# Hybrid attention and short-conv block on one core: keys held once, the normed input in a ring of slices, query tiles up and down in turn, merge from the last block

## The chip, the core and the metric

The kernel runs on one core of a Trainium2 chip. The metric is the device time of one execution in microseconds (us). Three timed runs of the kernel before gave 1969.12, 1975.21 and 1975.68 us, median 1975.21. TensorE (PE) does matrix products, VectorE (DVE) and ScalarE (ACT) work element by element, GpSimd (POOL) makes masks here, and SyncE (SP) issues every DMA, in order, from one program. Data lie in HBM, in on-chip SBUF (128 partitions) and in eight PSUM banks of 128 x 512 float32.

## The reference

```
h = RMSNorm(x)                                     # x: 2048 x 1024
q,k,v,z_att,b,c,u,z_conv,g_att,g_conv = split(h @ W_in)
A: 4 value heads; each has two query/key heads of width 64, partial rotary on q and k
   a = softmax(q1 k1^T / 8) - lam * softmax(q2 k2^T / 8), masked by position // 64
   att = RMSNorm(a @ v) * (1 - 0.2) * silu(z_att);      y_att = att @ W_att_out
B: y_conv = (b * conv3_causal(c * u) * silu(z_conv)) @ W_conv_out
m = sigmoid(g_att + bias0) * y_att + sigmoid(g_conv + bias1) * y_conv
out = x + RMSNorm(m @ W_out)
```

All is float32. Each operand of a large product is held as two reduced-precision parts, hi and lo (value minus hi), and a product is three matmuls: hi*hi, hi*lo, lo*hi. A score product packs the two parts into the 128 contracted rows (64 rows each), so two matmuls give all four part products.

## The kernel before, in words

The sequence has 4 blocks of 512 positions (NB) or 16 tiles of 128 (NT). There are four stages, and the order within each engine is fixed by the code.

1. **Norm and v.** x is loaded tile by tile (two buffers), normed, transposed by PE, split, and kept as `ht0` to `ht3`, one per block. w_v comes in four pieces through the two buffers `raw`. For each tile PE makes v (24 matmuls of 512 columns) and stores it to HBM.
2. **Projections.** 28 weight tiles `p` (z, conv, then q and k), each over the four blocks b = 0 to 3: 24 matmuls each (`split_product`), PSUM bank 4*(p%2)+b. ACT and DVE split the results, SP stores them (`qk_s`, `z_s`, `cv_s`). During the conv tiles, weights that are needed later are split into `split_s` in HBM: 16 gate tiles, 8 of the two output projections, 8 of W_out. `ht1` to `ht3` are stored to `ht_s`.
3. **Attention with gates between.** The work goes over TILES = 64 pairs (value head `pair`, query tile), G = 16*pair + tile, tiles upwards in every pair. Keys seen grow with the tile (`keys(G)`), in chunks of 512. In round R (-1 to 67) PE does the scores of G = R+1, the transposes of G = R-1, and in even rounds the product with v for two tiles. Between these steps stand *gate units* (`gates`, the fill): 64 units of 24 matmuls with h as the moving operand, whose results go to `gate_s`. `Plan` sets how many fill matmuls a round has, from column counts of PE (`tensor_columns`) and DVE (`vector_columns`). The first LEAD = 60 fill matmuls stand ahead of round -1. A unit needs its 1 MB weight (`w0`/`w1` in turn, loaded when the unit before the last is done) and h of its block, one buffer `ht0`: when block bb changes (units 16, 32, 48), `load_ht` reloads it in four pieces as the last unit frees them. `k_sl[c]` holds for each chunk the keys twice, in partitions 0-63 and again in 64-127, so one chunk takes 8 DMAs; `q_st` holds four tiles.
4. **Merge**, blocks b = 0 to 3. For m = 0 to 7 PE makes two half sums (`y_done`; 12 matmuls each, banks 0-3); gates come from HBM into `ring` (4 buffers), ACT takes the sigmoid, DVE multiplies, adds, ACT makes `m_hi` and DVE `m_lo`. Then 8 outputs of W_out (`f_done`; 24 matmuls each, banks 4-7), the norm, the residual and the store. `wa`, `br` (branch results) and `wo` are loaded after stage 3.

## Time and profile before

| | |
|---|---|
| median of three timed runs | 1975.21 us |
| profiled execution, and its span | 1981.93 us, 1980.1 us |
| PE busy | 1784.4 us (90%) in 8512 matmuls |
| DVE, ACT, POOL busy | 895.5, 583.5, 89.1 us |
| DMA | 345.66 MB, mean 175 GB/s |
| mean granted clock of PE | 0.953 of 2.4 GHz |

The span is first work to last work; 1.8 us of the profiled time lie around it. A busy share is an average: PE is the engine that is nearly always busy, so what counts is where it is idle and where its clock is at the lower level. "Idle before" or "waited for" names what ended an idle time.

### The profile page before, as it was taken

To read this page: it belongs to the slowest core of one execution; us is meant where nothing else is said; L and a number is where in the kernel's file an instruction comes from. 1 tells how busy PE (TensorE), PEld (TensorE's weight loads), DVE (VectorE), ACT (ScalarE), POOL (GpSimd) and SP (SyncE) were. 2 spreads that over 40 slices of the span, in tenths; PEclk is the share of its full clock that TensorE was granted. 3 is DMA by queue.
4 is the path that set the end of the run, shared out by engine and by line. 5 is a ranking of instruction groups with operands and counts; after the bars stand their busy time and mean duration, and the time that the engine had idled before them with its cause. 6 is when DMAs were issued, how large, how long until landed. Compare 5 with 4: busy or idle time off the path is not lost.

```text
span 1980.1 us, 22286 instructions
## 1 busy us (share of the span) xinstructions
PE 1784.4 (90%) x8512; PEld 1481.4 (75%) x8512; DVE 895.5 (45%) x1903; ACT 583.5 (29%) x1040; POOL 89.1 (5%) x74
## 2 busy tenths in 40 slices
PE   5999999999999992999899889978998279999998
PEld 4878888888888881788688778867887267777776
DVE  4546243535443310566466646744665032423232
ACT  5412112112112110344344434433444022323131
POOL 0000000000000000110111111101100000000000
PEclk8999999999999996999999989988999689999999
DMA  5557346566555349555864795497532944343432
GB/s 191 160 192 305 113 175 217 181 193 200 180 194 168 117 117 208 178 164 184 243 203 150 187 264 164 135 214 237 160 123 87 381 140 164 96 160 96 162 95 84
DMA packets 142853, 345.66 MB, mean 175 GB/s; under 512 B 14225, under 2 KB 51089, under 8 KB 127121
## 3 DMA queue, kind: packets, MB, share of 16 engines
q1 hardware_dynamic: 142738, 344.15, 55.6%
q8 instruction: 69, 1.13, 0.2%
q14 instruction: 46, 0.38, 0.1%
HBM read 224.55 MB, written 119.55 MB: 174 GB/s over the span
## 4 chain that ended last, share of the span: by engine, by line
PE 73%; DMA 12%; SPq 5%; ACT 4%; DVE 3%; issue 2%; DVEq 0%; ACTq 0%
PE bank L831 15%; PE bank L711 15%; PE bank L712 15%; PE bank L713 15%; DMA ring<-gate_s 6%; PE bank L797 5%; DMA w<-split_s 3%; PE bank L770 3%; PE bank L769 3%; PE bank L780 2%; DMA ht<-ht_s 1%; DMA post_w<-in_post_norm_w 1%; SPq L517 1%; SPq L519 1%; ACT ring L1069 1%
## 5 line engine op out<-in xcount | busy, mean ns | idle before, releaser
L831 PE MATMUL bank<-ht,w 128*128 128x512 f32 x1536 | 404.4, 406 | 78.5 <-DMA w<-split_s 50.9
L831 PEld LDWEIGHTS bank<-ht,w 128*128 128x128 f32 x1536 | 289.0, 195 | 139.9 <-DMA w<-split_s 53.1
L711 PE MATMUL bank<-ht,w 128*128 128x512 f32 x896 | 349.3, 390 | 2.9 <-ACT w L937 2.9
L712 PE MATMUL bank<-ht,w 128*128 128x512 f32 x896 | 349.0, 390 | 0.0
L713 PE MATMUL bank<-ht,w 128*128 128x512 f32 x896 | 349.0, 390 | 0.0
L711 PEld LDWEIGHTS bank<-ht,w 128*128 128x128 f32 x896 | 168.6, 188 | 38.3 <-ACT w L937 3.3
L712 PEld LDWEIGHTS bank<-ht,w 128*128 128x128 f32 x896 | 168.6, 188 | 35.0
L713 PEld LDWEIGHTS bank<-ht,w 128*128 128x128 f32 x896 | 168.5, 188 | 35.1
L1005 ACT ACTIVATE e<-e,nbias 128x128 f32<-128x128 f32 (+15 forms) x128 | 152.8, 1197 | 132.8 <-DVE nbias L1311 132.8
L1302 DVE CUSTOM_DVE_ANT_0 e<-bank,zeros 128x512 f32<-128x512 f32 x192 | 124.8, 687 | 107.5 <-PE bank L770 106.8
L711 PE MATMUL bank<-br,wa 128*128 128x512 f32 x256 | 102.9, 402 | 59.5 <-DVE ring L1385 32.0
L1336 DVE TENSOR_TENSOR at_lo<-bank,at_hi 128x512 fp32r<-128x512 f32 (+3 forms) x160 | 97.1, 607 | 87.3 <-ACT at_hi L1014 87.2
L1014 ACT ACTIVATE at_hi<-bank 128x512 fp32r<-128x512 f32 (+3 forms) x160 | 83.2, 527 | 164.0 <-PE bank L780 163.9
L769 PE MATMUL bank<-k_sl,q_st 128*128 128x512 f32 (+3 forms) x320 | 125.9, 398 | 0.9 <-DMA k_sl<-qk_s 0.9
L797 PE MATMUL bank<-at_hi,v_sl 128*128 128x256 f32 (+1 forms) x576 | 117.8, 283 | 9.0 <-DVE at_lo L1336 8.9
L711 PE MATMUL bank<-wo,m_hi 128*128 128x512 f32 x256 | 104.8, 409 | 16.8 <-DVE m_lo L1390 16.8
L701 POOL TENSOR_SCALAR mask<-kc,qc 128x128 f32<-128x128 f32 (+1 forms) x64 | 87.6, 1368 | 638.9 <-DVE mx L1302 625.6
L770 PE MATMUL bank<-k_sl,q_st 128*128 128x512 f32 (+3 forms) x320 | 115.0, 364 | 0.0
L1302 DVE CUSTOM_DVE_ANT_0 e<-bank,mask 128x128 f32<-128x128 f32 (+3 forms) x128 | 58.1, 489 | 124.5 <-PE bank L770 124.2
L797 PEld LDWEIGHTS bank<-at_hi,v_sl 128*128 128x128 f32 x576 | 95.3, 190 | 18.1 <-DVE at_lo L1336 15.9
L711 PEld LDWEIGHTS bank<-br,wa 128*128 128x128 f32 x256 | 49.2, 192 | 74.2 <-issue 54.7
L712 PE MATMUL bank<-wo,m_hi 128*128 128x512 f32 x256 | 103.3, 404 | 0.0
(135 smaller groups left out, 2385.4 us busy)
## 6 DMA issues: line engine op xcount, KB each, us to landing
w<-split_s SPq DMA_DIRECT2D x64, 1024.0 KB, 5.5
split_s<-piece SPq DMA_DIRECT2D x32, 1024.0 KB, 4.9
gate_s<-gate_st SPq DMA_DIRECT2D x64, 256.0 KB, 6.0
ring<-gate_s SPq DMA_DIRECT2D x64, 256.0 KB, 4.0
raw<-in_w_in SPq DMA_DIRECT2D x28, 512.0 KB, 6.2
ht_s<-ht SPq DMA_DIRECT2D x3, 4096.0 KB, 27.3
qk_s<-stage SPq DMA_DIRECT2D x24, 512.0 KB
k_sl<-qk_s SPq DMA_DIRECT2D x64, 192.0 KB, 10.8
```

Of the source, the lines that this page charges most:

```text
L701: nc.gpsimd.tensor_scalar(mask[m % 2][:, 0:wide], kc[:, c:c + wide], qc[:, G % NT:G % NT + 1], MASKED, ALU.is_gt, ALU.mult).then_inc(mask_ ...
L711: nc.tensor.matmul(out, left[0], right[0], start=start, stop=False)
L712: nc.tensor.matmul(out, left[0], right[1], start=False, stop=False)
L713: return nc.tensor.matmul(out, left[1], right[0], start=False, stop=stop)
L769: nc.tensor.matmul(out, q, k_sl[c // BLK][:, 0, h, 0:wide], start=True, stop=False)
L770: nc.tensor.matmul(out, q, k_sl[c // BLK][:, 1, h, 0:wide], start=False, stop=True).then_inc(qk_done, 1)
L797: return nc.tensor.matmul(bank[7][:, q0:QB], v, (at_lo if x == 1 else at_hi)[:, k, q0:QB], start=start, stop=stop)
L831: mm = nc.tensor.matmul(bank[2 + u % 2][:], w[u % 2][:, term // 2, k, :], ht[0][:, term % 2, k, :], start=i == 0, stop=i == PER_UNIT - 1)
L1005: nc.scalar.activation(e, e, ACT.Exp, bias=nbias[G % 2][:, h:h + 1], scale=SCALE, accum_out=esum[G % 2][:, h:h + 1]).then_inc(exp_done, 1)
L1014: nc.scalar.activation(at_hi[:, c // P:(c + wide) // P, q0:q0 + P], bank[5 + o % 2][:, 0:wide].rearrange("p (k n) -> p k n", n=P), ACT.Cop ...
L1302: nc.vector.tensor_tensor_reduce(e[:, c:c + wide], bank[(0, 1, 4)[o % 3]][:, 0:wide], mask[m % 2][:, 0:wide] if masked else zeros[:, 0:wid ...
L1336: nc.vector.tensor_tensor(at_lo[:, ks, q0:q0 + P], bank[5 + o % 2][:, 0:wide].rearrange("p (k n) -> p k n", n=P), at_hi[:, ks, q0:q0 + P]. ...
```

## The change

- **Keys once.** `k_sl[c]` has hi in partitions 0-63 and lo in 64-127 (2 DMAs of 256 KB a chunk). The queries are doubled instead: `q_st` has (hi, hi) and (lo, lo), for two tiles, 4 DMAs of 128 KB every second round. The matmuls are as many. `qk_s` is laid out by head, so stores of q and k tiles are cut at head bounds (`segments`: 3 or 4 DMAs in place of one).
- **h in a ring.** `ht_s` is stored in slices by k; `h_slot` puts slice k of block bb at place (8*bb+k) % 14. Six slices of the next block are loaded during units 1, 3, ... 11 of the block, two in its last unit.
- **Query tiles downwards in pairs 2 and 4 of heads** (`Plan.tile`): 0..15, 15..0, 0..15, 15..0. Chunks of k and v are replaced at their last use (`last_use`).
- **Stage change.** q and k tiles are projected in the order 0, 4, 1, 5, ...; the last two tiles go block by block, b = 1, 2, 3, 0, and loads for stage 3 are issued between their stores. The first two gate weights have places of their own (`first_w`); LEAD is 48.
- **Merge** runs over blocks 3, 2, 1, 0 (`n` counts them); `wa` 0-3 and `br` are loaded during stage 3. `ring` has 5 buffers. W_out is no longer split in stage 2 (24 pieces, not 32): it is loaded raw in the first merge block, ACT makes `wo_hi` and DVE `wo_lo`, one k for each m. The first two outputs take k = 0 to 5 first and 6, 7 after.
- **Start.** x has four buffers, w_v four of its own; the first projection weight's hi part is made before the last two copies of v on ACT.

The core of the diff:

```
-K_IN, V_IN, Q_IN = 8 * 16, 2 * 16, 4 * 16
+K_IN, V_IN, Q_IN = 2 * 16, 2 * 16, 4 * 16
...
+SEQ = [(p, b) for p in range(LINE - 2) for b in range(NB)] + [
+    (p, b) for b in (1, 2, 3, 0) for p in (LINE - 2, LINE - 1)]
...
+    def tile(self, G):
+        pair, i = divmod(G, NT)
+        return pair, (NT - 1 - i if pair % 2 else i)
...
+    def last_use(self, G, c):
+        return self.uses(G, c) and (G % NT == NT - 1 or not self.uses(G + 1, c))
...
-        return n + 2000
+        return n + (5000 if R >= TILES - 2 else 2000)
...
+        def h_slot(bb, k):
+            i = (KT * bb + k) % SLOTS
+            return ht[0][:, i] if i < KT else hx[i - KT][:]
...
+            for i, (p, b) in enumerate(SEQ[-2 * NB:]):
+                store_block(p, b)
+                if i == 1:
...
+                    load_q(Plan(True), 0)
+                    load_k(0, 0)
+                    load_q(Plan(True), 1)
+                if i == 3:
+                    sp.wait_ge(proj_done, AT[LINE - 1, 2] + 1)
+                    load_unit(0)
+                    load_v(0, 0)
+                    load_unit(1)
+                    for c in range(BLK, S, BLK):
+                        load_k(0, c)
+                if i == 6:
+                    sp.wait_ge(proj_done, AT[LINE - 2, 0] + 1)
+                    load_unit(2)
+                    for c in range(BLK, S, BLK):
+                        load_v(0, c)
...
+                        if g % 2 == 1 and g < 12 and bb < NB - 1:
+                            load_h(bb + 1, g // 2)
...
```

In the merge, `ring_load` of SP waits for what last used the place (a store, the sum, or the lo part), and wa 4 to 7 go out between the first gates:

```
+                if g >= 0:
+                    was_n, was = divmod(g, USES)
+                    if was >= 2 * KT:
+                        sp.wait_ge(y_stored[place], 16 * rows_before(n, i))
+                    elif was % 2:
+                        sp.wait_ge(m_sum, was_n * KT + was // 2 + 1)
+                    else:
+                        sp.wait_ge(m_lo_done, was_n * KT + was // 2 + 1)
...
+            for i in range(RING):
+                ring_load(0, i)
+                if i < 4:
+                    load_wa(4 + i)
```

On ACT behind `m_hi`, then on DVE behind `m_lo`, then PE's outputs:

```
+                    if n == 0:
+                        act.wait_ge(wo_in[m // 2], 32)
+                        nc.scalar.activation(wo_hi[m][:], wo_raw[m][:], ACT.Copy).then_inc(wo_hi_done, 1)
...
+                    if n == 0:
+                        dve.wait_ge(wo_hi_done, m + 1)
+                        nc.vector.tensor_tensor(wo_lo[m][:], wo_raw[m][:], wo_hi[m][:].bitcast(F32), ALU.subtract
+                                                ).then_inc(wo_lo_done, 1)
...
+                for o in range(2):
+                    rows(o, range(KT - 2))
+                for o in range(2):
+                    rows(o, range(KT - 2, KT))
```

**Stage change, SP's program.** Before, the stores of the last projection tile (stage to qk_s) and what follows (w a gate weight, q_st queries, numbers are buffers):

```order
L505 DMA w0<-split_s 128x2048
L484 DMA qk_s<-stage0 128x2x512
L484 DMA qk_s<-stage1 128x2x512
L484 DMA qk_s<-stage2 128x2x512
L484 DMA qk_s<-stage3 128x2x512
L505 DMA w1<-split_s 128x2048
L517 DMA q_st0<-qk_s 16x2x512
L519 DMA q_st0<-qk_s 48x2x512
```

In the changed kernel, behind the store of block 2 of the last tile (first_w the first two gate weights, k_sl keys by chunk, v_sl values):

```order
L608 DMA qk_s<-stage2 32x2x512
L608 DMA qk_s<-stage2 48x2x512 x2
L654 DMA first_w0<-split_s 128x2048
L638 DMA v_sl0<-v_s 128x4x128 x2
L654 DMA first_w1<-split_s 128x2048
L632 DMA k_sl1<-qk_s 64x2x512 x2
L632 DMA k_sl2<-qk_s 64x2x512 x2
L632 DMA k_sl3<-qk_s 64x2x512 x2
L608 DMA qk_s<-stage3 32x2x512
```

Before, one weight was loaded ahead of the last tile's stores, and behind them stood another, and then 8 rows for q, 32 for k, 8 for v and one for kc. Now loads stand between the stores of blocks 1, 2 and 3 (the first queries, chunk 0 of k and kc behind block 1), with those of block 0 still to come.

**First change of head pair, SP's program.** Before (ht0 is h, gate_st a unit's result, z_in a small load for the norm of v products):

```order
L564 DMA ht0<-ht_s 128x2x1024 x4
L505 DMA w1<-split_s 128x2048
L556 DMA gate_s<-gate_st0 128x512
L611 DMA z_in0<-z_s 128x256
L517 DMA k_sl0<-qk_s 16x2x512
L519 DMA k_sl0<-qk_s 48x2x512
```

The last two forms stand there 16 times in turn, over k_sl0 to k_sl3, before the next weight. Now:

```order
L697 DMA ht0<-ht_s 128x1024 x2
L751 DMA z_in0<-z_s 128x256
L632 DMA k_sl0<-qk_s 64x2x512 x2
L632 DMA k_sl1<-qk_s 64x2x512 x2
L654 DMA w1<-split_s 128x2048
L693 DMA gate_s<-gate_st0 128x512
L632 DMA k_sl2<-qk_s 64x2x512 x2
L632 DMA k_sl3<-qk_s 64x2x512 x2
L647 DMA q_st1<-qk_s 64x2x256 x4
```

Eight issues for k in place of 32, a weight load between them, and a quarter of h left to load in place of all.

**First merge block, DVE's program.** Before, the end of stage 3 (o_n, o_st: the last v product, normed and split) and the first m of the merge:

```order
L1345 SCALAR_TENSOR_TENSOR o_n<-bank,sub_w,o_r 128x256
L1349 TENSOR_TENSOR o_n<-o_n,z_in 128x256
L1353 TENSOR_TENSOR o_st<-o_n,o_st 128x256
L366 UNCONDITIONAL_BRANCH
L1385 TENSOR_TENSOR ring<-bank,ring 128x512 x2
L1388 TENSOR_TENSOR ring<-ring 128x512
L1390 TENSOR_TENSOR m_lo<-ring,m_hi 128x512
```

Now:

```order
L1559 SCALAR_TENSOR_TENSOR o_n<-bank,sub_w,o_r 128x256
L1563 TENSOR_TENSOR o_n<-o_n,z_in 128x256
L1567 TENSOR_TENSOR o_st<-o_n,o_st 128x256
L473 UNCONDITIONAL_BRANCH
L1598 TENSOR_TENSOR ring<-bank,ring 128x512 x2
L1601 TENSOR_TENSOR ring<-ring 128x512
L1603 TENSOR_TENSOR m_lo<-ring,m_hi 128x512
L1607 TENSOR_TENSOR wo_lo<-wo_raw,wo_hi 128x1024
```

A row for W_out has come in after each m, ahead of the multiplications of the next.

## Rows read from the trace of the kernel before

**Rows 1.** The page, part 1: busy time, share of the span, instructions.
```profile
PE 1784.4 (90%) x8512; PEld 1481.4 (75%) x8512; DVE 895.5 (45%) x1903; ACT 583.5 (29%) x1040; POOL 89.1 (5%) x74
```
**Rows 2.** PE's waits by releaser, whole span: line, total us, times, longest.
```profile
PE bank L831 <- DMA w<-split_s: 50.9, 5, 36.8
PE bank L711 <- DVE ring L1385: 32.0, 8, 26.5
PE bank L831 <- DMA ht<-ht_s: 27.6, 6, 13.0
PE bank L711 <- DMA br<-cv_s: 27.4, 1, 27.4
...
PE bank L797 <- DVE at_lo L1336: 8.9, 10, 1.6
```
**Rows 3.** Windows: length, busy and count of each engine, PE clock, DMA share, GB/s.
```profile
200.00:250.00 50.00, 50.00 (x222) 41.40 (x221) 10.93 (x14) 6.85 (x9) 0.00 (x0) 1.00 0.39 131
...
966.80:973.60 6.80, 3.31 (x8) 2.64 (x9) 1.85 (x6) 1.86 (x6) 0.00 (x0) 0.50 1.03 356
...
1369.60:1373.00 3.40, 3.40 (x8) 2.64 (x9) 0.00 (x0) 0.60 (x1) 0.00 (x0) 0.50 1.05 367
795.00:1525.00 730.00, 681.28 (x3707) 577.64 (x3708) 452.24 (x1277) 310.33 (x601) 85.72 (x62) 0.96 0.60 180
...
1683.00:1973.00 290.00, 271.61 (x1148) 219.07 (x1147) 97.62 (x168) 74.45 (x136) 0.00 (x0) 0.96 0.39 116
```
**Rows 4.** Timeline, PE, start: start, length, instruction, idle before.
```profile
23.98 1.97 PE L721 MATMUL bank<-ident,x_n 128*128 128x128 f32 x8 [10.05 <-DVE x_n L1103]
```
**Rows 5.** Timeline, ACT, start: the last of the four w_v pieces.
```profile
19.02 1.06 ACT L915 ACTIVATE wv_hi<-raw 128x1024 fp32r<-128x1024 f32 x1 [1.86 <-DMA raw<-in_w_v]
```
**Rows 6.** Timeline, DVE, at the first projection weight.
```profile
129.64 2.36 DVE L1138 TENSOR_TENSOR w<-raw,w 128x1024 fp32r<-128x1024 f32 x2 [0.25 <-ACT w L937]
```
**Rows 7.** Timeline, PE, stage 2 to stage 3.
```profile
741.75 5.60 PE L831 MATMUL bank<-ht,w 128*128 128x512 f32 x24
750.78 7.40 PE L831 MATMUL bank<-ht,w 128*128 128x512 f32 x24 [3.42 <-DMA w<-split_s]
794.98 5.13 PE L831 MATMUL bank<-ht,w 128*128 128x512 f32 x12 [36.80 <-DMA w<-split_s]
```
**Rows 8.** Timeline, SP, same place: key and weight loads.
```profile
751.45 0.43 SPq L517 DMA_DIRECT2D k_sl<-qk_s  x1
...
783.92 0.82 SPq L505 DMA_DIRECT2D w<-split_s  x2
```
**Rows 9.** The chain that ended last: start, length, what; pair changes, merge entry.
```profile
954.74 15.51 DMA w<-split_s
...
1130.71 22.55 DMA w<-split_s
...
1570.21 25.12 DMA post_w<-in_post_norm_w
```
**Rows 10.** The page, part 6: DMA issues, KB each, median us to landing.
```profile
w<-split_s SPq DMA_DIRECT2D x64, 1024.0 KB, 5.5
...
ring<-gate_s SPq DMA_DIRECT2D x64, 256.0 KB, 4.0
...
k_sl<-qk_s SPq DMA_DIRECT2D x64, 192.0 KB, 10.8
```
**Rows 11.** Timelines at the merge's entry, PE, then SP.
```profile
1527.63 1.63 PE L831 MATMUL bank<-ht,w 128*128 128x512 f32 x6
...
1535.92 0.92 SPq L581 DMA_DIRECT2D wa<-split_s  x2
```
**Rows 12.** Timeline, ACT, one m of merge block 2: sigmoids, then hi.
```profile
1803.01 1.51 ACT L1069 ACTIVATE ring<-ring,bias 128x512 f32<-128x512 f32 x2 [4.26 <-DMA ring<-gate_s]
1804.42 0.61 ACT L1079 ACTIVATE m_hi<-ring 128x512 fp32r<-128x512 f32 x1
```
**Rows 13.** Timeline, DVE, one lo part of m.
```profile
1604.45 0.69 DVE L1390 TENSOR_TENSOR m_lo<-ring,m_hi 128x512 fp32r<-128x512 f32 x1 [3.77 <-ACT m_hi L1079]
```

More of the change, by code:

```diff
@@ L287, in build @@
+        room.close()
         early.close()
         late = ExitStack()
[L291 to L297 removed]
@@ new lines, in late_wo_hi, with late_wo_lo, late_ring @@
+        def late_wo_hi(k):
+            wo_hi[k] = held(f"wo_hi{k}", [P, D], F32R, late)
+        def late_wo_lo(k):
+            sub = ExitStack()
+            wo_raw[k] = held(f"wo_raw{k}", [P, D], F32, sub)
+            sub.close()
+            wo_lo[k] = held(f"wo_lo{k}", [P, D], F32R, late)
+        def late_ring(i):
+            ring[i] = held(f"ring{i}", [P, BLK], F32, late)
+        for m in (4, 5, 6, 7, 0, 1):
+            late_wa(m)
+        m_hi = held("m_hi", [P, KT, BLK], F32R, late)
@@ new lines, in build @@
+        late_ring(0)
+        late_ring(1)
+        for k in (4, 5, 6):
+            late_br(k)
+        late_ring(2)
+        late_ring(3)
+        late_br(2)
+        late_br(3)
+        late_wo_hi(0)
+        late_wo_lo(0)
+        for k in (7, 0, 1):
+            late_br(k)
+        m_lo = held("m_lo", [P, KT, BLK], F32R, late)
+        late_wo_hi(1)
+        late_wo_lo(1)
+        late_ring(4)
+        post_w = held("post_w", [P, D], F32, late)
+        late_wa(2)
+        for k in (2, 3, 4):
+            late_wo_hi(k)
+            late_wo_lo(k)
@@ L675, in _ @@
+            for place, s_ in enumerate(y_stored):
+                sp.wait_ge(s_, 16 * rows_before(NB, (place - NB * USES) % RING))
         @block.gpsimd
@@ L786, in values @@
                     B = G // 2
-                    last = plan.keys(G) // P - 1
+                    last = max(plan.keys(G - 1), plan.keys(G)) // P - 1
                     pe.wait_ge(at_lo_done, plan.before(G) + c // BLK + 1)
@@ L1287, in _ @@
             dve.wait_ge(fills_ready, 2)
+            for s_ in stored:
+                dve.wait_ge(s_, 16 * stores_before(LINE))
             def attend(plan):
```

910 lines of the change are left out of this document (495 added, 415 removed).

## The prediction, as put on record before the changed kernel ran

> **What bounds the kernel now.** The page comes first: PE is busy 1784.4 of 1980.1 us in 8512 matmuls, twice as long as DVE [rows 1]. The change neither adds nor removes a matmul, so it can only take idle time and slow clock from PE. PE's waits show where the idle time lies: three kinds end on DMAs for weights, h and branch results, one on DVE in the merge [rows 2]. Windows then give the size for each stage. Undisturbed, 222 matmuls of 512 columns pass in 50 us, 0.225 us each, at clock 1.00; I use 0.227 [rows 3].
>
> Lost time, stage by stage:
>
> - Start: one gap of 10.05 us before the third tile's transposes [rows 4]. Stage 2 itself is full.
> - Stage 2 to 3: gaps of 3.42 and 36.80 us. Behind them the clock is at its lower level (1.2 GHz): 24 fill matmuls took 7.40 us in place of 5.60, and 12 took 5.13 where 2.9 are due. Together 40.2+1.8+2.2 = 44.2 [rows 7].
> - Attention (795 to 1525): 730.0-681.3 = 48.7 idle. In five stretches of this stage (first and last shown) the clock is 0.50 while PE is busy for 27.9 us; at 2.4 GHz half would do, so 13.9 more. Together 62.6 [rows 3].
> - Merge: fill ends at 1529.3 [rows 11], and the products of the first block at 1683.0, where the last window begins. A block is 384 matmuls, 87.2 us at 0.227. So the first block loses 153.7-87.2 = 66.5, and the other three 290-261.6 = 28.4, or 9.5 each [rows 3].
>
> **The change part by part.**
>
> *Start.* The last piece of w_v ended at 20.1 on ACT, after a wait for its DMA [rows 5], and the norm of the third tile is queued behind it. With places of their own, nine loads (4.5 MB) go out at once. At the bulk rate of 0.36 MB/us (below) they need 12.5 us plus some 2.5 to start and land, so that piece begins at 15.1, not 19.0. I take 3.9 (0 to 6). The first projection weight: its hi part comes earlier, but DVE's lo part at 129.64 had waited only 0.25 us for ACT [rows 6], so what remains is DVE's queue; 0.3. Sum 4.2.
>
> *Stage 2 to 3.* Before, w for the third unit was issued at 783.9, behind 49 issues for q, k, v and kc at 0.43 us or more [rows 8]. Now the last eight projection blocks take 8 x 5.45 = 43.6 us. The first two weights are issued after the fourth, some 20 us before PE needs them, with 4 MB in that batch (11 us). The third weight follows after the seventh block with 1.5 MB of v, 2.5 MB or 7 us, while the first two units last 48 x 0.227 = 10.9. The last stores queue behind these loads; they hold ACT and DVE up, not PE, whose banks for these tiles were emptied two tiles before. DVE's new wait for all stores (what is queued behind it is the first score maximum, due after the two units) ends about 7 us after the last block, also inside 10.9. Smaller q/k stores, 3 or 4 for one, cost SP about 0.4 us each, beside 5.45 us blocks. I leave 2 us (0.5 to 10): 42.2 gained.
>
> *Attention.* Before, at a change of head pair, 32 key issues kept SP for 15 us and the next weight went out behind them, landing 15.51 and 22.55 us later [rows 9] against 5.5 at the median [rows 10]; h could be fetched only as its buffer came free. Now h is 3/4 loaded ahead. The changes of h block and of pair fall in rounds 14 to 17 and 46 to 49, where the new order puts two long tiles side by side: round 17 has 12,464 columns of its own by the plan and 43 fill matmuls of 512, 15.3 us at 0.227 for 512, and keys are reloaded one such round before use. A score step cannot lose much there. One tight place is made: between pairs 2 and 3 the tiles are short. Key chunk 0 is replaced in round 30, just behind two h slices (1 MB, 2.9 us), and is wanted one round later, 4.3 us by its columns. Bounds: nothing, if it lands as soon as 256 KB of gates, 4.0 us, and 7 if as late as keys did, 10.8 [rows 10]; I take 3.5 with its clock. About 7 us of the waits for at_lo (8.9 in all, rows 2) stay, since no step there is changed. So 10.5 stay of 62.6 (4 to 35): 52.1 gained.
>
> *Merge, first block.* Before, wa, br, ring, wo and post_w, 4+8+1+8+0.5 = 21.5 MB, went out from 1535.9 [rows 11]; post_w landed at 1595.3 [rows 9]: 0.36 MB/us. DVE waited for it although it needs it only for outputs; that wait moves behind the m loop. Now let T be the end of the fill. br and wa 0 to 3 are there, and PE can start about 3 us after T (the jump out of the plan's branch). SP must see the last gate store landed, T+5. Then 5 gates and 4 wa alternate: the fourth gate stands behind 4.0 MB and lands at T+18; ACT needs it before the first m_hi (0.61), then m_lo (0.69) is at T+20 [rows 12, 13]. Only then does the sixth gate go out and with it the first two pieces of W_out: 1.5 MB, 4.1+2 us, T+26. ACT's copy (1.06, as rows 5) and DVE's subtraction (1.2, as rows 6) stand ahead of the second m's multiplications, which therefore come at T+29. PE needs their banks from T+19 on, so it waits about 10 us. After that, each m takes 5.5 to 6.8 us (one gate load, sigmoid, hi, lo, copy, subtraction) against PE's 5.45, and the outputs start at about T+58, 14 after the 43.6 that eight m cost. With 5 us of slow clock the block loses 19 (8 to 45): 66.5-19 = 47.5 gained. If post_w and W_out's copies hid as well as they did in stage 2, nothing of the 10 would be there.
>
> *Later blocks.* Before, the cycle of one m was: lo part, issue, two gates landing (4.26 waited), two sigmoids (1.51), hi, lo, 6.4 us with the gaps [rows 12], for 5.45 of PE, and the last lo parts came 5 to 7 us after PE wanted them. With five buffers one gate of each m is loaded ahead, so the one that is waited for lands about 0.7 us sooner (256 KB at 0.36), 3.6, and one sigmoid is off the path: 3.6+0.75+0.61+0.69+0.3 = 5.9. The first lo part comes some 12 us in (the fourth gate's place holds an output row that has to be normed and stored first), the seventh 6 x 5.9 later at 47, the eighth, which needs no load, about 3.4 on (two products, sum, hi, lo), 51. PE is done with the half sums at 43.6 and now has 36 output matmuls (8.2 us) that need only m = 0 to 5: it comes to the last two at 51.8. One us a block stays (0 to 4): 25.4 gained.
>
> **Sum.** 4.2+42.2+52.1+47.5+25.4 = 171.4; 1980.1-171.4 = 1808.7, and 1.8 outside the span: 1810.5. The profiled execution took 1981.9 and the median of the timed runs is 6.7 lower; with that, 1803.8. I forecast 1803.
>
> **Rivals.**
>
> *Pair changes still wait.* For: in one round SP issues 8 v loads (2 MB) behind 4 of q, and any weight behind 2.5 MB lands 7 us later. Against: a unit lasts 8.6 us even in that dense round 17 (15.3 x 24/43), and a weight needs 5.5. If 45 of the 62.6 stay, 35 more: 1838.
>
> *The first merge block is bound by the W_out chain.* For: ACT and DVE work in order and both now wait for a DMA that waits for them. Against: after the first two m the pieces are ahead. If each m costs 3 us more, 24 more: 1827.
>
> *Slower: weight loads fall behind everywhere.* Mechanism: q comes in 128 KB loads with rows of 1 KB, each round has more issues, and the one queue delays every one of 64 weights. A unit lasts 730/62 = 11.8 us; a load hurts only when it lands later than its unit's end. To be slower than before, PE must lose 172/64 = 2.7 us a unit, that is a mean landing of 14.5 us in place of 5.5. At 3.0 a unit: 1803+192 = 1995. Against it: DMA share 0.60 in this stage [rows 3] with half the key bytes now. The Trainium skill speaks against such loads (DMA: Bandwidth & Descriptors, Bandwidth: batch DMAs to 1 MiB or more, since smaller ones stay well under peak). That is this rival; where only weights were in flight the trace shows 367 GB/s at full share [rows 3].
>
> *It does not take effect*: the waits move to other loads in the same queue and less than 10 us is gained, 1970.
>
> **Chances.** Forecast (1780 to 1820) 0.65; pair changes 0.13; first merge block 0.12; slower 0.03; no effect 0.01; better than 1780 (residues at their lower ends, 12.5 for 34.5 us, give 1781; below that, waits that I count as fixed go too) 0.06. Range 1775 to 1840 for 8 in 10. Half a per cent is about what a measurement of this kernel can tell from no change: faster 0.96, within 0.01, slower 0.03.
>
> **What would show it.** Right: PE idle under 100 us in all; no wait above 5 us between stage 2 and 3; fewer than five low-clock stretches in attention; a wait of about 10 us for DVE's ring at the third or fourth m of the first merge block; no m_lo waits later. Wrong: w waits of several us spread over attention; a gap behind k in round 31 above 7; merge blocks of 95 us.

## The result, and the profile after

Four timed runs of the changed kernel gave 1841.49 to 1842.56 us, median 1842.26; before stood at 1975.45 beside them. The ratio is 0.9326 (95% interval 0.9298 to 0.9354): 6.7% faster. The forecast was 1803 us with a range of 1775 to 1840. The direction is right, the time is 2 us outside the range, and the gain is 133 us where 172 were forecast. The profiled execution spans 1840.3 us against 1980.1.

The page of the changed kernel, part 1 (compare [rows 1]):

```profile
PE 1761.2 (96%) x8512; PEld 1469.3 (80%) x8512; DVE 891.5 (48%) x1903; ACT 581.8 (32%) x1040; POOL 89.0 (5%) x74
```

The matmuls are as many; their busy time fell by 23 us, as less of it ran at the lower clock level (mean granted clock 0.986, before 0.953). PE's waits, whole span (compare [rows 2]):

```profile
PE bank L899 <- DVE x_n L1306: 16.6, 2, 10.2
PE bank L889 <- DVE ring L1598: 13.6, 1, 13.6
PE bank L975 <- DVE at_lo L1550: 11.9, 16, 2.2
PE bank L947 <- DVE stage L1427: 8.3, 1, 8.3
PE bank L947 <- DMA k_sl<-qk_s: 7.2, 1, 7.2
PE bank L947 <- DVE mx L1514: 6.1, 1, 6.1
PE bank L1010 <- DMA w<-split_s: 5.1, 4, 2.3
```

The waits for h and for branch results are gone, and that for weights fell from 50.9 to 5.1 us. New are two waits at the stage change (L1427, L1514); the one for keys was 0.9 us before. The one at L1598 in the first merge block had 26.5 us before (L1385, [rows 2]). Windows of PE by stage (columns as in [rows 3]):

```profile
738.00:776.00 38.00, 22.41 (x86) 17.98 (x85) 6.64 (x24) 6.40 (x16) 3.63 (x2) 0.78 0.79 219
775.00:1455.00 680.00, 656.84 (x3643) 558.20 (x3642) 442.65 (x1258) 307.07 (x588) 81.97 (x60) 0.99 0.66 203
1467.90:1573.00 105.10, 91.17 (x387) 74.61 (x388) 39.44 (x58) 31.93 (x53) 0.00 (x0) 0.92 0.62 204
1573.00:1833.00 260.00, 260.00 (x1149) 215.29 (x1148) 97.61 (x168) 72.84 (x138) 0.00 (x0) 1.00 0.41 129
...
1108.20:1115.00 6.80, 4.76 (x15) 4.19 (x16) 3.07 (x13) 0.80 (x2) 1.57 (x1) 0.50 0.47 112
```

The last row is one of six stretches at the lower clock level from the stage change to the end of the first merge block (three in attention, PE busy for 11.6 us in them; two at the stage change, 8.3 us busy; one in the merge). Half of that busy time counts as lost, as in the prediction. Lost time by stage, in us:

| | lost before | lost after | gained | forecast |
|---|---|---|---|---|
| start (third tile's transposes at 20.51, before 23.98) | | | 3.5 | 4.2 |
| stage 2 to 3: 38.0-22.4 idle, 4.1 clock | 44.2 | 19.7 | 24.5 | 42.2 |
| attention: 680.0-656.8 idle, 5.8 clock | 62.6 | 29.0 | 33.6 | 52.1 |
| first merge block: 105.1-87.2 | 66.5 | 17.9 | 48.6 | 47.5 |
| later blocks: 290 us before, 260 now | 28.4 | 0 | 30.0 | 25.4 |
| sum | | | 140.2 | 171.4 |

The later blocks take 260.0 us where 0.227 a matmul gives 261.6, so 30.0 are gained from a loss put at 28.4. The spans differ by 139.8, so the table leaves out next to nothing. (From the fill's end to the second block's first product the first merge block takes 152.8 and 105.1 us; so 1 of its 48.6 us belongs to the row below.) Two rows carry the miss: 17.7 at the stage change and 18.5 in attention.

### The profile page after: what moved, and what is told of

Read it like the earlier page. It is cut to its first block, busy times and chain, and to the rows that moved or that the text cites. A ratio compares the mean times of both kernels' runs of the same rounds, so it can differ in the third digit from the quotient of the medians.

```text
span 1840.3 us, 22425 instructions
## 1 busy us (share of the span) xinstructions
PE 1761.2 (96%) x8512; PEld 1469.3 (80%) x8512; DVE 891.5 (48%) x1903; ACT 581.8 (32%) x1040; POOL 89.0 (5%) x74
## 4 chain that ended last, share of the span: by engine, by line
PE 83%; DMA 6%; SPq 4%; ACT 3%; DVE 2%; issue 2%; DVEq 0%; ACTq 0%
PE bank L889 18%; PE bank L890 18%; PE bank L891 18%; PE bank L1010 15%; PE bank L975 5%; PE bank L947 3%; PE bank L948 3%; PE bank L958 2%; ACT e L1205 2%; DMA gate_s<-gate_st 1%; SPq L638 1%; DMA qk_s<-stage 1%; DMA ring<-gate_s 1%; PE bank L899 1%; DVE at_lo L1550 1%
## 5 line engine op out<-in xcount | busy, mean ns | idle before, releaser
L889 PE MATMUL bank<-ht,w 128*128 128x512 f32 x896 | 349.3, 390 | 2.6 <-issue 2.6
L890 PE MATMUL bank<-ht,w 128*128 128x512 f32 x896 | 349.3, 390 | 0.0
L891 PE MATMUL bank<-ht,w 128*128 128x512 f32 x896 | 349.1, 390 | 0.0
L1010 PE MATMUL bank<-ht,w 128*128 128x512 f32 x912 | 239.9, 398 | 1.2 <-DMA w<-split_s 1.2
L889 PEld LDWEIGHTS bank<-ht,w 128*128 128x128 f32 x896 | 168.5, 188 | 38.1 <-ACT w L1118 3.0
L891 PEld LDWEIGHTS bank<-ht,w 128*128 128x128 f32 x896 | 168.6, 188 | 35.1
L890 PEld LDWEIGHTS bank<-ht,w 128*128 128x128 f32 x896 | 168.5, 188 | 35.0
L1010 PEld LDWEIGHTS bank<-ht,w 128*128 128x128 f32 x912 | 168.5, 191 | 33.9 <-DMA w<-split_s 1.4
L1514 DVE CUSTOM_DVE_ANT_0 e<-bank,zeros 128x512 f32<-128x512 f32 x192 | 125.0, 688 | 130.4 <-PE bank L948 129.9
L1205 ACT ACTIVATE e<-e,nbias 128x128 f32<-128x128 f32 (+15 forms) x128 | 152.8, 1196 | 83.7 <-DVE nbias L1523 83.5
L1010 PE MATMUL bank<-hx,w 128*128 128x512 f32 x576 | 156.1, 399 | 3.9 <-DMA w<-split_s 3.9
L947 PE MATMUL bank<-k_sl,q_st 128*128 128x512 f32 (+3 forms) x320 | 129.3, 408 | 21.6 <-DVE stage L1427 8.3
L975 PE MATMUL bank<-at_hi,v_sl 128*128 128x256 f32 (+1 forms) x576 | 117.9, 283 | 12.0 <-DVE at_lo L1550 11.9
L1010 PEld LDWEIGHTS bank<-hx,w 128*128 128x128 f32 x576 | 105.5, 190 | 25.0 <-DMA w<-split_s 5.6
L878 POOL TENSOR_SCALAR mask<-kc,qc 128x128 f32<-128x128 f32 (+3 forms) x64 | 87.5, 1367 | 619.9 <-DVE mx L1514 619.3
L948 PE MATMUL bank<-k_sl,q_st 128*128 128x512 f32 (+3 forms) x320 | 117.1, 370 | 0.0
L889 PE MATMUL bank<-br,wa 128*128 128x512 f32 x256 | 101.0, 395 | 14.3 <-DVE ring L1598 13.6
L1550 DVE TENSOR_TENSOR at_lo<-bank,at_hi 128x512 fp32r<-128x512 f32 (+3 forms) x160 | 97.1, 607 | 31.2 <-ACT at_hi L1214 30.8
L890 PE MATMUL bank<-br,wa 128*128 128x512 f32 x256 | 100.7, 394 | 0.0
L891 PE MATMUL bank<-br,wa 128*128 128x512 f32 x256 | 100.5, 393 | 0.0
```

What stands on the lines that cost most here:

```text
L878: nc.gpsimd.tensor_scalar(mask[m % 2][:, 0:wide], kc[:, c:c + wide], qc[:, plan.tile(G)[1]:plan.tile(G)[1] + 1], MASKED, ALU.is_gt, ALU.mu ...
L889: nc.tensor.matmul(out, left[0], right[0], start=start, stop=False)
L890: nc.tensor.matmul(out, left[0], right[1], start=False, stop=False)
L891: return nc.tensor.matmul(out, left[1], right[0], start=False, stop=stop)
L947: nc.tensor.matmul(out, q_st[G // 2 % 2][:, 0, h, qs], k, start=True, stop=False)
L948: nc.tensor.matmul(out, q_st[G // 2 % 2][:, 1, h, qs], k, start=False, stop=True).then_inc(qk_done, 1)
```

## Where the stage change loses its time

PE, then ACT, of the changed kernel between stages 2 and 3 (compare [rows 7]; start, length, instruction, idle before):

```profile
738.79 11.04 PE L1010 MATMUL bank<-ht,first_w 128*128 128x512 f32 x48
758.08 0.47 PE L947 MATMUL bank<-k_sl,q_st 128*128 128x128 f32 x1 [8.25 <-DVE stage L1427]
...
760.42 2.50 PE L1010 MATMUL bank<-ht,w 128*128 128x512 f32 x5 [1.23 <-DMA w<-split_s]
...
769.46 0.58 PE L947 MATMUL bank<-k_sl,q_st 128*128 128x256 f32 x1 [6.11 <-DVE mx L1514]
```

```profile
748.44 1.09 ACT L1180 ACTIVATE stage<-bank 128x512 fp32r<-128x512 f32 x2 [23.38 <-DMA qk_s<-stage]
756.71 0.60 ACT L1180 ACTIVATE stage<-bank 128x512 fp32r<-128x512 f32 x1 [7.18 <-DMA qk_s<-stage]
```

The last projection ends at 738.8, but ACT writes its last output at 756.7: tiles 26 and 27 write the same `stage` buffer one after the other, and ACT waits for the landing of a store. SP's queue (compare [rows 8]) shows why it lands late:

```profile
728.70 1.52 SPq L654 DMA_DIRECT2D first_w<-split_s  x1
730.26 3.95 SPq L632 DMA_DIRECT2D k_sl<-qk_s  x6
734.26 18.62 SPq L608 DMA_DIRECT2D qk_s<-stage  x9
753.23 0.34 SPq L654 DMA_DIRECT2D w<-split_s  x1
753.62 7.56 SPq L638 DMA_DIRECT2D v_sl<-v_s  x6
761.23 1.76 SPq L608 DMA_DIRECT2D qk_s<-stage  x3
```

The store of block 3 of tile 26 is issued at 734.3 behind 4 MB of weights, v and keys, and the chain of waits has it landing 12.99 us after its last issue. The very last stores stand behind 2.5 MB more and end at 767.8; only then may DVE take the first score maximum, which PE waits for at 769.46. The wait before it, 8.25 us, is for DVE's last output: the first score products are written to PSUM banks that the last two projection tiles filled, and PE's program waits for that output ahead of them.

## The experiments

All are edits of the changed kernel, timed in five rounds. The median of before, run beside them, was 1975.56 to 1976.04 us in every group, so medians are compared across groups; differences under 2 us are not told apart.

**The changed kernel again.** 

> The changed kernel itself, unaltered, on the chip and beside the runs that the next ones are compared with. Expected by every theory: 1842 us, with 1841 to 1844 as its range, so that what the others gain or lose can be read against it.

Measured: 1840.65 us. This is the base below.

**Loads behind the last stores.**

```
-                    for c in range(BLK, S, BLK):
-                        load_k(0, c)
...
-                    for c in range(BLK, S, BLK):
-                        load_v(0, c)
             load_unit(3)
+            for c in range(BLK, S, BLK):
+                load_k(0, c)
+                load_v(0, c)
```

> Key and value chunks 1 to 3 of the first head pair (3 MB) are loaded behind everything else of the stage change instead of ahead of the last stores. Theory (queue): PE's 15.6 us of idle time between stage 2 and 3 and the slow clock behind it come from the last stores, which stand in the one queue behind 4.0 and 2.5 MB of loads. With 1.5 MB less ahead of it and six issues fewer, the store of block 3 of tile 26 lands some 8 us sooner, at about 741 us, DVE's last output comes at about 746 and its wait for all stores ends at about 751, where PE ends its first two units at 750: 12 to 18 us gained, 1826 us. Rival (reuse): tiles 26 and 27 write the same stage buffer one right after the other, so each of the last blocks waits for a full landing whatever stands in the queue; then under 5 us are gained, 1838 us.

Measured: 1841.01 us, no gain. PE and ACT of this kernel show that the two waits did shrink, and a third came:

```profile
756.41 0.39 PE L946 MATMUL bank<-k_sl,q_st 128*128 128x256 f32 x1 [2.74 <-DVE mx L1513]
...
777.46 0.69 PE L974 MATMUL bank<-at_hi,v_sl 128*128 128x256 f32 x2 [9.42 <-DVE at_lo L1549]
```

```profile
774.89 0.60 ACT L1242 ACTIVATE gate_st<-bank 128x512 f32<-128x512 f32 x1 [13.44 <-DMA gate_s<-gate_st]
```

The wait of 8.3 us is gone and the one for the first maximum fell from 6.1 to 2.7. But the 12 issues now moved behind the stores held SP until 766, and the first gate's store was issued only at 767.54. ACT waits for it with the attention's copies queued behind. The store of block 3 landed at 739.8 (expected 741); DVE's last output was there at 749.7 and its first maximum started at 756.1 (expected 746 and 751). The gain was wrong above all because one more user of the queue had been overlooked.

**Blocks in twos.**

```
-    (p, b) for b in (1, 2, 3, 0) for p in (LINE - 2, LINE - 1)]
+    (p, b) for bs in ((1, 2), (3, 0)) for p in (LINE - 2, LINE - 1) for b in bs]
...
-                if i == 1:
+                if i == 2:
```

> The last eight projection blocks go in the order 26/1, 26/2, 27/1, 27/2, 26/3, 26/0, 27/3, 27/0, so that a stage buffer is used again two blocks later; the loads keep their size and are issued after the third and fourth block and, for the third weight, after the seventh. Theory (queue): the 4 MB batch now goes out one block sooner and the store of tile 26, block 3, lands at about 738 us, two outputs already made behind it; half or more of the stall goes, 8 to 16 us, 1830 us. Rival (reuse): as much or more, 12 to 20 us, 1826 us. If both this run and the one with the stores ahead gain, it takes both, late stores and an early reuse, to make the stall; if this one gains nothing, reuse is no part of it.

Measured: 1838.86 us, 1.8 less; neither theory's gain. The waits of PE in this kernel:

```profile
PE bank L1010 <- DMA w<-split_s: 10.2, 4, 6.7
...
PE bank L947 <- DVE mx L1514: 6.3, 1, 6.3
PE bank L947 <- DVE stage L1427: 0.9, 1, 0.9
```

The wait for the outputs fell to 0.9 and the one for the third weight rose to 6.7. So early reuse of the buffer is one way in which the late stores reach PE; with it gone, they reach PE through the weight, which was issued only at 750.3, behind them.

**Keys and values spread over rounds.** As the first edit, but only key chunk 1 follows `load_unit(3)`, and in `attend`:

```
+                late = {1: (1, 2), 5: (2, 3), 9: (3, NB)} if plan.causal else {}
...
+                    if R in late:
+                        load_v(0, late[R][0] * BLK)
+                        if late[R][1] < NB:
+                            load_k(0, late[R][1] * BLK)
```

> As in the run with the stores ahead, but of the chunks of keys and values that the first tiles don't use only key chunk 1 is loaded right away; the other five (2.5 MB, 10 issues) go out in the rounds before they are wanted. Theory (one queue): putting the same loads behind the stores moved the stall to the next thing that stood behind them, the store of the first gate, which came 9.6 us late to the attention. With the loads spread, that wait goes as well: of the stall of 20 us (8.4, 1.5 and 6.4 us of idle time and the slow clock) about 3 to 8 stay, 1829 us. Rival (start-up chain): after DVE's first score maximum the exponentials, the transposes and the lo part take their time whatever the queue does, and PE has too few fill matmuls in the first rounds to cover it; then the wait at about 768 us stays near 9 us and the time near 1839 us.

Measured: 1835.08 us, 5.6 less, between the two. PE of this kernel:

```profile
755.89 0.58 PE L954 MATMUL bank<-k_sl,q_st 128*128 128x256 f32 x1 [3.25 <-DVE mx L1521]
...
768.56 0.44 PE L982 MATMUL bank<-at_hi,v_sl 128*128 128x256 f32 x2
...
775.27 3.43 PE L1017 MATMUL bank<-ht,w 128*128 128x512 f32 x8 [1.98 <-DMA w<-split_s]
```

The value product starts at 768.6 and not, as with the loads behind the stores, at 777.5, and has no idle time before it: the start-up chain is not the limit, the queue was. Idle time of 1.2, 3.3 and 2.0 us stays of 15.6. The profiled execution of this one spans 1829.8 us, 10.5 less than the changed kernel's; the median shows only half of that.

**Keys ahead of the fill's loads of the same step.** `gates(part)` on SP moved behind the block that calls `load_k`.

> At each step of the attention the load of the next pair's keys is issued before the fill matmuls' own loads, so that in round 30 key chunk 0 goes out ahead of two h slices of 1 MB in all and the weight. Theory: the 7.2 us that PE waits for this chunk at 1103 us is the queue ahead of it (2.9 us of h, 2.0 us of issues, and the weight); at least 5 of the 7.2 go, and about 3 us of slow clock with them: 7 to 10 us, 1833 us. Rival: the landing of 256 KB takes 7 to 9 us in this stage whatever stands ahead, and what is gained is the issue time, 2 us: 1840 us.

Measured: 1841.32 us, nothing. The edit missed its place: the two h slices belong to the round before and were still issued first, at 1098.7 and 1099.0, the keys at 1100.3 and 1100.9. It tells nothing of the theory.

**The last h slices behind the keys.** `load_h` of slices 6 and 7 for block 2 moved out of `gates`:

```
                                 load_k(pair + 1, score[0])
+                                if pair == 1 and c == 0:
+                                    last_h(1)
```

> The last two h slices of the third h block (1 MB) are loaded behind key chunk 0 of the third pair, in round 30, and not ahead of it at the end of round 29. (The run before that put keys ahead of the fill's loads of the same step left this order as it was, since the h loads belong to the round before.) Theory: these 2.9 us of transfer and 1 us of issue are ahead of the chunk; the wait of 7.2 us at 1103 us shrinks to 3 to 4 us, and the slow clock behind it may go: 4 to 7 us gained, 1836 us. Rival: 256 KB of keys in rows of 2 KB take 6 us or more to land by themselves; 1 to 2 us gained, 1840 us.

Measured: 1838.97 us. The chain of waits has this landing at 7.97 us after issue in place of 9.50, and PE's wait is 4.85 in place of 7.22:

```profile
1107.54 0.48 PE L953 MATMUL bank<-k_sl,q_st 128*128 128x128 f32 x1 [4.85 <-DMA k_sl<-qk_s]
```

So up to 2.4 us of the wait come from the h ahead; the runs that left this place alone had waits of 6.3 to 7.4 us there. The time is 1.7 less, which is not told apart from nothing. The rival is nearer.

**Tiles upwards.**

```
-        return pair, (NT - 1 - i if pair % 2 else i)
+        return pair, (NT - 1 - i if pair == VH - 1 else i)
```

> Query tiles run upwards in the first three head pairs and downwards in the last alone. The first two changes of pair then go from the longest tile to the shortest, with all four value chunks loaded after the last tile is done and wanted a round later, and the third change goes from longest to longest. Theory: the wait for key chunk 0 at 1103 us with its slow clock goes (10 us gained), and each of the two other changes costs 5 to 10 us for values and weights behind 2 MB of values: 1842 to 1854 us, 1848 us. Rival: the order of the tiles is what made the attention faster than before, and its changes cost 15 us or more each as they did there: 1865 us. Second rival: the order brings nothing, and only the wait at 1103 us goes: 1832 us.

Measured: 1833.34 us, 7.3 less, which is the second rival. PE's waits in the attention (770 to 1458) of this kernel:

```profile
PE bank L975 <- DVE at_lo L1550: 11.9, 13, 2.0
PE bank L1010 <- DMA w<-split_s: 5.5, 4, 3.1
```

The wait for keys is gone, with its slow clock, and a change from the longest tile to the shortest costs only weight waits of up to 3.1 us. The downward order in the second pair is a loss here.

**32 key issues.** Each `load_k` from the second pair on cut into four times as many DMAs (64 KB each; the expectation has 32 by mistake).

> From the second pair on each key load is cut into four (32 KB pieces of 16 rows of two heads), so that a change of pair has 32 key issues as before the change, at the same bytes as now. Theory: what made the changes of pair cheap is that they are spread by the order of tiles; 6 more issues a chunk cost SP some 3.6 us, beside rounds of 10 us or more, and are felt only at chunk 0 of the third pair: 3 to 8 us slower, 1846 us. Rival: the number of key issues was the cost, 15 us of SP at each change: 25 us or more slower, 1868 us.

Measured: 1844.63 us, 4.0 more. The theory's size holds: with the new order and h ahead, the number of issues costs little. The wait for key chunk 0 stayed at 7.0, so the price is spread and not where I put it.

**h at the end of a block.**

```
-                    if g == GATE_TILES - 1 and i == 5 and bb < NB - 1:
+                    if g == GATE_TILES - 1 and i % 6 == 5 and bb < NB - 1:
                         sp.wait_ge(ht_free, bb + 1)
-                        for k in (6, 7):
+                        for k in (i // 6 * 2, i // 6 * 2 + 1):
                             load_h(bb + 1, k)
...
-                        if g % 2 == 1 and g < 12 and bb < NB - 1:
-                            load_h(bb + 1, g // 2)
```

> No h slice of the next block is fetched ahead: all eight (4 MB) are loaded during the last unit of a block, two at each quarter of it, as before the change. Theory: neither the order of tiles nor the number of key issues made the attention faster (the runs before this showed them worth -8 and 4 us), so it was the h ring, and without it the 27.6 us that PE waited for h before the change come back, less what the smaller key traffic frees: 15 to 27 us slower, 1862 us. Rival: with fewer issues in the queue the slices land within their unit (8 to 11 us), and it is under 8 us slower, 1846 us.

Measured: 1845.72 us, 5.1 more: the rival. PE waited for h 2.8 us in all.

**Two and three of these at once.** First upwards with 32 issues, then all three.

> Tiles upwards in the first three pairs and 32 key issues at a change of pair, h ring kept. Theory (cover): with four key chunks at once behind the longest tile, 24 more issues hold SP for 15 us and the weight behind them comes late: 8 to 15 us slower than the changed kernel, 1853 us. Rival (additive): -8 and +4, 1838 us.

> All three at once: tiles upwards in the first three pairs, 32 key issues at a change of pair, and h loaded during the last unit of a block. What is left of the change in the attention is that keys are stored once and q comes by pairs of tiles. Theory (cover): each of the three hides what the others would cost, so that one alone undone showed -8, +4 and +4 us; with all gone a change of pair and of h block fall together again and 25 to 35 us of the attention's gain go, 1870 us. Rival (additive): -8, +4 and +4 make nothing, 1842 us, and the gain comes from what is left.

Measured: 1836.52 us and 1854.77 us. PE's waits in the attention (770 to 1484) with all three:

```profile
PE bank L1010 <- DMA w<-split_s: 10.5, 4, 3.4
PE bank L1010 <- DMA ht<-ht_s: 7.3, 3, 3.1
...
PE bank L1010 <- DMA hx<-ht_s: 4.5, 1, 4.5
```

Order and issues add (-7.3 and +4.0 make -3.3; measured -4.1). h does not: loaded late it costs 5.1 us with the tiles in turn and 18.3 with the tiles upwards (1854.77 against 1836.52; that pair also has 32 key issues). So there is cover: late h is cheap with the tiles in turn and 8 key issues, and dear with the tiles upwards and 32. Whether the order or the issues make it dear is not shown, since no run had late h with only one of them. What is shown is that with h fetched ahead the order in turn brings nothing and costs its wait for keys.

**W_out's split two m later.** On ACT, and likewise on DVE:

```
-                        act.wait_ge(wo_in[m // 2], 32)
-                        nc.scalar.activation(wo_hi[m][:], wo_raw[m][:], ACT.Copy).then_inc(wo_hi_done, 1)
+                        for k in ((m - 2,) if 2 <= m < KT - 1 else (m - 2, m - 1, m) if m == KT - 1 else ()):
+                            act.wait_ge(wo_in[k // 2], 32)
+                            nc.scalar.activation(wo_hi[k][:], wo_raw[k][:], ACT.Copy).then_inc(wo_hi_done, 1)
```

> In the first merge block the copy and the subtraction that split W_out's piece k stand two m later in ACT's and DVE's order; loads as they are. Theory (W_out chain): the wait of 13.7 us for DVE's product at 1484 us is the landing of the first piece, 1495.1, and what follows it; without it DVE can make that product right after the first lo part, 1487.6, so PE waits about 4 us: 9 to 12 us gained with the clock, 1831 us. Rival (gates): the sixth and later gates are asked for only after the first lo part and land 4 to 6 us later, behind W_out in the same queue; the gap only moves to the next m, and under 4 us are gained, 1839 us.

Measured: 1841.21 us, nothing, as the rival had it. The wait of 13.6 us became 4.5, and two new ones stand at the end of the block:

```profile
1525.85 0.50 PE L889 MATMUL bank<-wo_hi,m_hi 128*128 128x512 f32 x1 [2.10 <-DVE wo_lo L1609]
...
1530.64 0.80 PE L889 MATMUL bank<-wo_hi,m_hi 128*128 128x512 f32 x1 [3.83 <-DVE wo_lo L1609]
```

The last lo part did come earlier, at 1528.4 and not 1535.3, but my edit heaps three splits behind it. With the **first five gates ahead of the four weights** as well:

> As the run with W_out's split two m later, and besides the first five gates (1.25 MB) are loaded ahead of the weights of m 4 to 7 (4 MB), not in turn with them. Theory: the fourth gate then lands some 9 us sooner, at about 1476 us in place of 1485.6, the first lo part is made at about 1479 and PE, which wants its fifth bank at 1479 to 1484, waits for nothing; the weight of m 4 is wanted at 1492 and lands before it. The block's loss of 18 us falls to 3 or less: 15 us gained, 1827 us. Rival: W_out and the later gates now stand behind those 4 MB in one piece, until about 1487, and hold up m 3 or 4 by as much: 6 to 8 us gained, 1835 us.

Measured: 1839.71 us, less gain than even the rival. The first lo part came at 1480.1, 6.8 earlier, the second only at 1491.4 (the sixth gate behind the 4 MB), and the heap stayed.

**The merge paced.** Five gates, wa 4, then per m two gates, one weight of m 5 to 7 and W_out's pieces as they are used; splits with `for k in ((), (), (0, 1), (2, 3), (4,), (5,), (6,), (7,))[m]`.

> First merge block: five gates first, then the weight of m 4, those of m 5 to 7 one at a time behind later gates, W_out's pieces in the order and at the pace of their use, and their splits at m 2 (two), 3 (two), 4, 5, 6 and 7, so that none stands in a heap behind the last lo part as it did when all stood two m later. Theory (chain of lo parts): the block ends when the last of eight lo parts is there, each 6 us behind the one before; the first now comes at about 13 us after the fill's end in place of 20, and no 4 MB stand between the sixth gate and its landing, so the last comes at about 56 in place of 68 us and PE needs it at 52: of 18 us lost about 6 to 9 stay, 1832 us. Rival: as in the last two runs the gain is given back at the end of the block, 1839 us or more.

Measured: 1832.99 us, 7.7 less, the theory's 1832. The window of the block, PE's waits for DVE's products in it, and DVE's last lo part:

```profile
1467.90:1563.00 95.10, 89.60 (x385) 73.08 (x386) 39.25 (x58) 31.27 (x51) 0.00 (x0) 0.98 0.66 224
PE bank L890 <- DVE ring L1600: 5.5, 2, 4.0
```

```profile
1525.76 0.69 DVE L1605 TENSOR_TENSOR m_lo<-ring,m_hi 128x512 fp32r<-128x512 f32 x1 [0.70 <-ACT m_hi L1280]
```

The block takes 95.1 us in place of 105.1. In the changed kernel PE, held for 13.6 us, came to the outputs when nearly all they need was there (0.3 us of waiting); with that wait cut alone, it came early and waited at the end. The paced form joins an early first lo part, no 4 MB ahead of the sixth gate and no heap behind the last lo part.

**Output rows in order** (`for o in range(2 * QPB): rows(o, range(KT))`) and **a ring of four** (`RING = 4`).

> Merge: each group of output products takes all eight m at once, in order, and no longer the first six m of both halves of the first tile ahead of the last two. Theory: PE is through the half sums and six m of one group 47.7 us into a block, the last lo part comes at about 51 us, so PE waits 3 to 4 us in each of the three later blocks and slow clock may follow: 9 to 14 us slower, 1854 us. Rival: with the fifth buffer the lo parts are early enough, and nothing changes, 1842 us.

> Merge: the ring of gates and output rows has four buffers, not five (the fifth's memory stays empty). Theory: each gate load is asked for about half an m later, the lo parts follow 6.4 us apart in place of 5.9, the last comes some 4 us later in a block, and PE waits for it in every block: 12 to 20 us slower, 1858 us. Rival: the split of the output products is what hides the last lo parts, with 4 us to spare: under 4 us slower, 1844 us.

Measured: 1846.05 us and 1867.97 us. In order costs 5.4 us, between theory and rival, and all in the first block (110.3 us against 104.4 from its first product to the second block's); in the later blocks, where the theory had put it, PE waits for nothing. Four buffers cost 27.3 us, more than either had; 17 of them lie in the later blocks (276.9 us against 260.0) and most of the rest in the first. One lo part behind another in a later block, with five buffers and then with four:

```profile
1680.64 0.69 DVE L1603 TENSOR_TENSOR m_lo<-ring,m_hi 128x512 fp32r<-128x512 f32 x1 [2.67 <-ACT m_hi L1279]
1685.94 0.69 DVE L1603 TENSOR_TENSOR m_lo<-ring,m_hi 128x512 fp32r<-128x512 f32 x1 [2.68 <-ACT m_hi L1279]
```

```profile
1696.60 0.69 DVE L1603 TENSOR_TENSOR m_lo<-ring,m_hi 128x512 fp32r<-128x512 f32 x1 [3.71 <-ACT m_hi L1279]
1703.16 0.69 DVE L1603 TENSOR_TENSOR m_lo<-ring,m_hi 128x512 fp32r<-128x512 f32 x1 [3.94 <-ACT m_hi L1279]
```

5.3 us with five, just under PE's 5.45; 6.2 to 6.7 over all later blocks with four. The fifth buffer made the later blocks full. It accounts for 17 of the 30 us that they gained; with four buffers they still are 13 shorter than before, and which part of the change does that was not tried.

**What helped, together.** Spread keys and values, tiles upwards, and the first form of the merge edit, then its paced form:

> All that helped: keys and values of the first pair spread over the rounds, tiles upwards in the first three pairs, and both changes of the first merge block. The stalls lie in four places apart from each other, so the gains should add: 6.5 + 8 + 15 us from 1842, 1812 us. Rival: what is gained at one place comes back at another, since one queue serves all; then 1820 us or more.

> The paced merge block together with keys and values of the first pair spread over the rounds and tiles upwards in the first three pairs. The version without the paced block took 1827 us; theory: 9 us less, 1818 us. Rival: the gain of the block doesn't add, 1826 us.

Measured: 1827.03 us and 1815.45 us. The first gains 13.6 us where its parts alone gained 13.8 (5.6+7.3+0.9), so nothing came back, though the time is the rival's. The second has a ratio to before of 0.9192 (0.9171 to 0.9213), 25 us less than the changed kernel beside a sum of the single gains of 20.6 (5.6+7.3+7.7). It is the fastest version here.

## Why the prediction was right or wrong

- **Start, right.** The last w_v piece was forecast at 15.1 and came at 15.55 ([rows 5] had 19.02); 3.5 us gained of 4.2.
- **Stage change, wrong.** The failed step is "they hold ACT and DVE up, not PE, whose banks for these tiles were emptied two tiles before", with DVE's wait for all stores ending "about 7 us after the last block". It ended 29 us after, at 767.8, and the banks that count are those of the first scores, which wait for DVE's last output. I had charged the loads between the stores with their bytes once each, from their issue, and asked whether each would be in time. I had not followed the stores that stand behind them: a store behind 4 MB (11 us by the bulk rate) holds the next output, which holds the next store, which then stands behind the next batch. Two such turns and the issues are the 29 us. PE has only two units, 11 us, to bridge them. The runs confirm the queue as cause, since the waits moved with the loads; spreading keys and values over the rounds, the best of three tries, brought back 5.6 of the 19.7 in the median (9 of 15.6 us of idle time in the profiled execution).
- **Attention, the size wrong and partly the reason.** What was wrong is "a score step cannot lose much" and the sum of 10.5 us left. The trace has at_lo 11.9 (forecast 7), keys 7.2 plus half of 4.8 us of slow clock (forecast 3.5 together; the landing took 9.5 us, nearer to its bound of 10.8 than to 4.0), weights 3.9 and the rest slow clock, neither in the sum. Part of it is the step that failed at the stage change once more, by the chain of waits at the first change of pair:

```profile
963.91 7.32 DMA gate_s<-gate_st
971.81 3.64 ACT e L1205 x4
976.27 0.70 DVE at_lo L1550
977.02 1.46 PE bank L975 x10
```

  A gate's store goes out behind eight loads of v (2 MB, issued from 955.5 to 963.0) and a weight and lands 7.32 us later (6.0 at the median), ACT waits 3.67 us for it with the exponentials behind, and PE 2.22 for at_lo. At the third change ACT waits 5.22 for such a store, at 1320.5. This is read from the trace; no run took those loads away. As to the reason: of 37 us by which the stage is shorter (697 from 734, windows of 3717 and 3728 matmuls), undoing order, issues and h ahead together gives back 17 (714; 14 in the medians). I counted on all three. One at a time, h ahead is worth 5.1 us, few issues 4.0, and the order costs 7.3; late h costs 18.3 when the other two are undone as well. What the other 20 us come from (keys stored once, smaller query loads) was not tried by itself and stays open.
- **First merge block, right in size and mechanism.** ACT at W_out's first piece, and PE's product that waits (changed kernel, compare [rows 12]):

```profile
1495.10 1.06 ACT L1282 ACTIVATE wo_hi<-wo_raw 128x1024 fp32r<-128x1024 f32 x1 [8.25 <-DMA wo_raw<-in_w_out]
```

```profile
1498.16 0.76 PE L889 MATMUL bank<-br,wa 128*128 128x512 f32 x1 [13.57 <-DVE ring L1598]
```

With T = 1467.3 forecast and trace are: first lo part T+20 and T+19.6, W_out's first piece T+26 and T+27.8, the second m's product T+29 and T+30.0, PE's wait from T+19 for 10 and from T+17 for 13.6; 17.9 us lost where 19 were forecast. The rival by which the W_out chain binds the block throughout was wrong. So was "If post_w and W_out's copies hid as well as they did in stage 2, nothing of the 10 would be there": the copies were moved, 4.5 us of the wait stayed, and the rest came back at the block's end.
- **Later blocks, right in sign, wrong in the cause.** I had lo parts 5.9 us apart, saved at the end by the split output products. They are 5.3 apart and, with five buffers, the split isn't needed there; it is in the first block.
- **Forecast from the profile to the median, wrong.** I took off 6.7 us since before's profiled execution lay that far above its median. After's lies within 0.2 us of its own (1842.11). Without that step the forecast would have been 1810.5.
- **Rivals.** "Pair changes still wait" was nearest in time (1838), for the wrong sum: the three changes of pair lose about 19.5 of the attention's 29.0 us (waits of 1.1+2.2, 7.2 and 2.3+1.0 with half of 11.6 us of slow clock), where it had 45 for the stage, and it has nothing at the stage change. "Slower" did not happen: weights still land 5.4 us after issue at the median, although queries come in 128 KB loads. The Trainium skill (DMA: Bandwidth & Descriptors, Bandwidth) warns of such loads; cutting keys to 64 KB pieces did cost 4 us here, so this case agrees in sign, and the price is small. Whether the smaller pieces or SP's 24 more issues a change make it is not separated. The 367 GB/s set against the rule was not quite of weights only: a gate's store of 256 KB and small loads were out beside them.
- **The signs.** PE idle under 100 us (79.1), fewer than five low-clock stretches in attention (three), a wait for DVE's ring at the fourth m (13.6) and no m_lo waits later came true. "No wait above 5 us between stage 2 and 3" did not (8.3 and 6.1), and one sign of being wrong came: the gap behind k was above 7 (7.2).

Together: 17.7 + 18.5 + 0.7 short, 5.7 more than forecast in the merge, and 6.7 for the offset: 1803.8 + 31.2 + 6.7 = 1841.7.

## What to carry to other kernels

Where one queue serves loads and stores, price a batch of loads by the stores behind it and by whoever waits for those, not only by whether the loads are in time. If one wait is taken out of a stretch in which several things share a queue or a chain, look at the stretch's end before counting the gain: the loads behind the stores, the blocks in twos and the first two merge edits all shrank the wait they aimed at and gained 0 to 2 us. Undo the parts of a large change one by one and in pairs: a part that looks cheap alone (late h, 5.1 us) can be dear without the others (18.3), and one part may be a pure cost.

## What the runs showed that was not expected

- Twelve key and value issues in a row took SP 15 us (751.5 to 766.4, loads behind the last stores), 1.2 us each, where a store of the projections takes 0.43 and a load of keys 0.6 in the same program. It happens with some MB outstanding; what makes the issues slow is not shown. The 256 KB store behind them went out 16 us after ACT had written its data (751.5).
- 256 KB of keys landed 7.97 us after issue with no h ahead of them (a weight was), where loads of gates of the same size take 3.4 us in the merge and their stores 6.0 at the median (the page's part 6).
- One ring buffer more (2 KB a partition) was worth 27 us, 17 of them in the later blocks, where it moves a cycle from about 6.4 to 5.3 us across PE's 5.45.
